# Norm boundaries of a two-layer block: another order on TensorE, ScalarE and VectorE, the next phase's first half k-outer

## Chip, core and metric

The kernel runs on one core of a Trainium2 chip. The metric is the time of the whole program on the device in microseconds (us); lower is better. The kernel before has a median of 2238.09 us over 3 runs.

## What is computed

The reference is a stack over x of 512 tokens by 1024 features, all in float32: an mLSTM mixer, a feed-forward layer, a gated spatial mixer, a feed-forward layer, then a second block with two attention branches and a convolved feed-forward layer. What matters here is what stands between any two of them:

```python
x = x + g1 * rmsnorm(y, norm_g[i, 1])
h = rmsnorm(x, norm_g[i, 2]) * (1.0 + sc2) + sh2
y = jnp.square(jax.nn.relu(h @ ffn_w1[i])) @ ffn_w2[i]
x = x + g2 * rmsnorm(y, norm_g[i, 3])
```

rmsnorm divides a token's row by the root of the mean of its squares plus 1e-6. So between the last product into y and the first product of h stand two norms in a row, each of which needs a sum over all 1024 features of a token.

## The kernel before

**Layout.** Activations are held transposed, as [128 partitions, 8 feature blocks, 512 tokens]: X (the residual), Y (the last blocks of y are summed here), h_hi and h_lo. Each float32 operand is split into a high part in a reduced format and a low rest, and each product is three matmuls (hi*hi, hi*lo, lo*hi). Weights come as 1 MB tiles of 256 columns into two slots raw[0] and raw[1], in turns. ScalarE copies a tile to its high part (`w_split`, line 1201; for the next phase's first two tiles `split_next`, line 1252, into buffers of their own) and VectorE subtracts to get the rest (`w_rest`, line 1711; `rest_of`, line 1767), which counts `split_done`.

**Queues.** The order of the work is written out by hand for each engine, with waits on counting semaphores. SyncE's queue issues the tiles in order (`tile_in`, line 368); a tile t waits for `split_done` of tile t-2, that is, until the rest of the tile that was in its slot has been computed. ScalarE and VectorE carry out their lists in order.

**A boundary.** There are five: a_out, ffn0, b_out, ffn1 and out2 (named by the phase that ends). All but out2 have two norms (`two`). The last two weight tiles of a phase are multiplied in `last_pair` (line 620), the first two of the next one in `first_pair` (line 665), or, behind ffn0, in a loop of its own (lines 933 to 950). Both split the tokens in halves of 256. In `last_pair` half 0 goes through four blocks m of 8 k steps of three products, into banks 0 to 3; then half 1 the same, into banks 4 to 7, and while half 1 is multiplied, the norms of half 0 are computed:

- VectorE's `y_out(half, m)` (line 1772) adds a block's bank to y; ScalarE squares it (`y_square`, line 1219) into T[m]; VectorE adds the square into sq_sum (`y_sum`, line 1787).
- TensorE's `sums` (line 598) multiplies sq_sum by a column of ones; `variance` (line 1796, VectorE), `half_power` (line 2536, GpSimd: the power -1/2), `diagonal` (line 1802, VectorE) and `spread_half` (line 615, TensorE) turn it into the reciprocal root of each token on all partitions, in a bank.
- `merge` (line 1810) computes x = x + y * gain * that, a block at a time. In half 1 GpSimd does every second add (line 2550). ScalarE squares x (`x_squares`, line 1235), `x_sums` (line 606) sums on TensorE, and the chain variance, power, diagonal, spread follows once more.
- `h_parts` (line 1825): VectorE scales a block of x into T, ScalarE makes h_hi (`hi`, line 1254), VectorE the rest h_lo (line 1829) and counts `h_ready`.

All the small products of the statistics stand at fixed places in TensorE's list: in `last_pair` those of half 0 at the steps (half, m, k) in the code, in the next phase's first half those of half 1, by `norm_step(name, i, k)` (line 652). `first_pair` runs s (the tile) outermost, then k, then two banks. Its half 1 waits for `h_ready1` k by k.

The lists of ScalarE and VectorE at the head of a boundary, which the change touches:

```python
split_next(0)                 # ScalarE, lines 1264 to 1268
for m in range(3):
    y_square(m, y[m], hs[0])
split_next(1)
y_square(3, y[3], hs[0])
```

```python
y_out(0, 2)                   # VectorE, lines 1851 to 1857
y_sum(0, 2)
y_out(0, 3)
y_sum(0, 3)
rest_of(t2, 1, next_w[name][1], 2, lambda: variance(0, 9 * kb_ + 1))
diagonal(0, 2 * kb_)
spread_done(0, 2 * kb_)
```

## Time and profile before

| | us |
|---|---|
| median of 3 runs | 2238.09 |
| lowest, highest | 2231.41, 2239.53 |
| the profiled execution's own time | 2227.2 |
| its span, first to last instruction | 2225.4 |
| TensorE busy | 2123.7 (95% of the span) |
| VectorE, ScalarE, GpSimd busy | 1230.6, 826.0, 95.9 |
| mean granted TensorE clock | 0.981 of full speed |

Matmuls are pipelined: the profile's duration of one is longer than the distance between two starts, so distances are read from starts. A float32 product with 128x1 or with `diag` shows as two records. "Idle before" is time in which the engine did nothing, with the instruction that ended it. Times of a row count from the start of the span; the boundaries stand at 266 to 348 (a_out), 668 to 737 (ffn0), 984 to 1053 (b_out), 1358 to 1422 (ffn1) and 1816 to 1866 us (out2).

### The profile page before, as it was taken

The numbers are of one execution on the slowest core, as the hardware profiler recorded it, in microseconds if no ns is written. First come the engines' busy times: TensorE is split into PE (matmuls) and PEld (weight loads), VectorE is DVE, ScalarE is ACT, GpSimd is POOL, SyncE is SP. The second block draws the span as 40 slices with busy tenths as digits, with TensorE's granted clock in tenths as the row PEclk, the third lists the DMA queues.
The fourth block names the chain that finished last, engine by engine and source line by source line (L and its number), as shares of the span: only waits on it lengthen the run. The fifth ranks groups of instructions, "written<-read, shape, count | busy, mean of one in ns | idle before, by whom it ended". The sixth has DMA issues, their size and how long they took to land.

```text
span 2225.4 us, 29809 instructions
## 1 busy us (share of the span) xinstructions
PE 2123.7 (95%) x11614; PEld 1777.6 (80%) x11614; DVE 1230.6 (55%) x1994; ACT 826.0 (37%) x1229; POOL 95.9 (4%) x71
## 2 busy tenths in 40 slices
PE   6999879999999999999999999999999999999997
PEld 5897768888888998788888888886666689888886
DVE  4666667666667445647333336535557756535455
ACT  3433334334244322325342343336445534424243
POOL 0000010000001002401000000100000000000000
PEclk9999989999999999999999999999999999999999
DMA  9451314666551432231223323222012131222221
GB/s 293 152 190 48 110 56 159 203 210 196 194 188 59 151 96 91 79 114 57 76 95 95 112 91 96 63 69 85 1 48 77 47 112 60 94 95 94 95 85 67
DMA packets 224630, 239.34 MB, mean 108 GB/s; under 512 B 6642, under 2 KB 219021, under 8 KB 223877
## 3 DMA queue, kind: packets, MB, share of 16 engines
q1 hardware_dynamic: 182757, 193.73, 27.1%
q10 hardware_dynamic: 41760, 44.06, 6.0%
q8 instruction: 76, 1.25, 0.2%
q14 instruction: 37, 0.30, 0.0%
HBM read 230.81 MB, written 6.31 MB: 107 GB/s over the span
## 4 chain that ended last, share of the span: by engine, by line
PE 66%; issue 18%; DVE 7%; DMA 3%; ACT 3%; DVEq 1%; POOL 1%; SPq 1%; ACTq 0%; POOLq 0%
PE bank L546 43%; PE bank L1133 4%; PE bank L686 2%; DMA ada_raw<-in_ada_w 2%; PE bank L740 2%; PE bank L644 2%; DVE ada_acc L1722 2%; PE bank L1081 1%; PE bank L1070 1%; PE bank L1028 1%; PE bank L1058 1%; PE bank L1104 1%; PE bank L1116 1%; ACT w_hi L1201 1%; PE bank L611 1%
## 5 line engine op out<-in xcount | busy, mean ns | idle before, releaser
L1711 DVE TENSOR_TENSOR w_lo<-raw,w_hi 128x2048 fp32r<-128x2048 f32 x137 | 314.6, 2296 | 246.2 <-ACT w_hi L1201 246.1
L546 PE MATMUL bank<-h_hi,w_hi 128*128 128x512 f32 x1056 | 413.7, 392 | 0.0
L546 PE MATMUL bank<-h_hi,w_lo 128*128 128x512 f32 x1056 | 411.7, 390 | 0.0
L546 PE MATMUL bank<-h_lo,w_hi 128*128 128x512 f32 x1056 | 411.6, 390 | 0.0
L1201 ACT ACTIVATE w_hi<-raw 128x2048 fp32r<-128x2048 f32 x147 | 280.1, 1905 | 314.4 <-PE bank L546 308.1
L546 PE MATMUL bank<-g_hi,w_hi 128*128 128x512 f32 x688 | 271.3, 394 | 9.4 <-DVE g_lo L2498 5.1
L546 PE MATMUL bank<-g_hi,w_lo 128*128 128x512 f32 x688 | 269.6, 392 | 0.0
L546 PE MATMUL bank<-g_lo,w_hi 128*128 128x512 f32 x688 | 269.4, 392 | 0.0
L546 PEld LDWEIGHTS bank<-h_hi,w_lo 128*128 128x128 f32 x1056 | 198.7, 188 | 41.6
L546 PEld LDWEIGHTS bank<-h_lo,w_hi 128*128 128x128 f32 x1056 | 198.8, 188 | 41.1 <-issue 0.2
L546 PEld LDWEIGHTS bank<-h_hi,w_hi 128*128 128x128 f32 x1056 | 198.7, 188 | 40.7 <-issue 0.2
L546 PEld LDWEIGHTS bank<-g_hi,w_hi 128*128 128x128 f32 x688 | 130.3, 189 | 37.7 <-DVE g_lo L2498 6.4
L546 PEld LDWEIGHTS bank<-g_hi,w_lo 128*128 128x128 f32 x688 | 130.1, 189 | 27.4
L546 PEld LDWEIGHTS bank<-g_lo,w_hi 128*128 128x128 f32 x688 | 130.2, 189 | 26.7
L1722 DVE SCALAR_TENSOR_TENSOR ada_acc<-ada_raw,c_act,ada_acc 128x256 f32<-128x256 f32 x280 | 135.8, 485 | 21.5 <-issue 0.6
L2197 DVE TENSOR_TENSOR g_lo<-tmp,g_hi 128x512 fp32r<-128x512 f32 (+1 forms) x72 | 44.5, 630 | 127.9 <-ACT g_hi L1454 127.8
L1448 ACT ACTIVATE tmp<-bank 128x512 f32<-128x512 f32 (+1 forms) x72 | 39.4, 547 | 163.7 <-PE bank L546 163.1
L546 PE MATMUL bank<-w_hi,h_hi 128*128 128x256 f32 x352 | 100.0, 284 | 0.0
L546 PE MATMUL bank<-w_lo,h_hi 128*128 128x256 f32 x352 | 99.6, 283 | 0.0
L546 PE MATMUL bank<-w_hi,h_lo 128*128 128x256 f32 x352 | 99.6, 283 | 0.0
L1906 DVE TENSOR_TENSOR y_acc<-y_acc,bank 128x512 f32<-128x512 f32 x60 | 40.8, 684 | 88.7 <-PE bank L546 88.7
L644 PE MATMUL bank<-g_hi,w_hi 128*128 128x256 f32 x256 | 78.5, 307 | 1.4 <-DVE w_lo L1711 1.1
(415 smaller groups left out, 3668.9 us busy)
## 6 DMA issues: line engine op xcount, KB each, us to landing
raw<-in_ffn_w SPq DMA_DIRECT2D x64, 1024.0 KB, 5.2
ada_raw<-in_ada_w ACTq DMA_DIRECT2D x40, 1024.0 KB, 5.2
raw<-in_w_up SPq DMA_DIRECT2D x22, 1024.0 KB, 5.0
raw<-in_b_w_in SPq DMA_DIRECT2D x16, 1024.0 KB, 5.3
raw<-in_w_in SPq DMA_DIRECT2D x15, 1024.0 KB, 5.6
raw<-in_a_w_in SPq DMA_DIRECT2D x12, 1024.0 KB, 5.5
ada_head<-in_ada_w SPq DMA_DIRECT2D x8, 1024.0 KB, 11.8
raw<-in_b_w_out SPq DMA_DIRECT2D x8, 1024.0 KB, 5.2
```

The lines of the kernel that those rows point to most:

```text
L546: mm = pe.matmul(o, x, y, start=(k == 0 and j == 0), stop=(k == kc - 1 and j == 2))
L611: mm = pe.matmul(bank[4 * half + 1][:, c:c + 1], xsq[:, b, c * P:c * P + P], ones[:, 0:1], start=(b == 0 and c == 0), stop=(b == KB - 1 an ...
L644: mm = pe.matmul(bank[4 * half + m][:, hs], x, y, start=(k == 0 and j == 0), stop=(k == KB - 1 and j == 2))
L686: mm = pe.matmul(o, x, y, start=(k == 0 and j == 0), stop=(k == KB - 1 and j == 2))
L740: mm = pe.matmul(bank[6][:], x, y, start=(k == 0 and j == 0), stop=(k == KB - 1 and j == 2))
L1133: mm = pe.matmul(bank[7][:], x, y, start=(k == 0 and j == 0), stop=(k == KB - 1 and j == 2))
L1201: act.activation(w_hi[s][:], raw[s][:], ACT.Copy).then_inc(sem("hi_done"), 1)
L1448: r = act.activation(t, i[:, hs], ACT.Relu)
L1711: dve.tensor_tensor(w_lo[s][:], raw[s][:], f32(w_hi[s][:]), ALU.subtract).then_inc(sem("split_done"), 1)
L1722: i = dve.scalar_tensor_tensor(o, src[:, k], c_act[:, k:k + 1], o, ALU.mult, ALU.add)
L1906: dve.tensor_tensor(y, y, bank[m][:], ALU.add).then_inc(sem(f"evac{m}"), 1)
L2197: return dve.tensor_tensor(g_lo[:, y, hs], T[m][:, hs], f32(g_hi[:, y, hs]), ALU.subtract)
```

## The change

It reorders the boundaries. Banks of the statistics are named by `norm_banks`: (0, 0, 1, 4) for half 0 and (5, 5, 6, 7) for half 1 where there are two norms. On TensorE the statistics move, `sums` takes the fourth square straight from T[3], and `x_sums` goes by pairs of blocks:

```diff
+def sums(name, half):
+    kb_, o = BOUNDS[name], bank[norm_banks(name, half)[0]]
+    for i, sq in enumerate([sqa, T[3]]):
+        if i == 0:
+            pe.wait_ge(sem(f"sq_ready{half}"), 5 * kb_ + 1)
+        else:
+            pe.wait_ge(sem("y_squared"), 12 * kb_ + 8 + 4 * half)
+        for c in range(2):
+            mm = pe.matmul(o[:, c:c + 1], sq[:, half * HALF + c * P:half * HALF + c * P + P],
+                           ones[:, 0:1], start=(i == c == 0), stop=(i == c == 1), skip_group_check=True)
     mm.then_inc(sem(f"sq_used{half}"), 1)
...
-                    sums(0, 9 * kb_, sqa)
-                if (half, m, k) == (1, 1, 2):
-                    spread_half(0, 2 * kb_)
-                if two and (half, m, k) == (1, 3, 2):
-                    x_sums(name, 0, range(4, KB))
-                if two and (half, m, k) == (1, 3, 7):
-                    spread_half(0, 2 * kb_ + 1)
+                if (half, m, k) == (1, 0, 3):
+                    sums(name, 0)
+                if (half, m, k) == (1, 0, 7):
+                    spread_half(name, 0)
+                if two and (half, m, k) == (1, 2, 2):
+                    x_sums(name, 0, (2, 3))
+                if two and (half, m, k) == (1, 2, 6):
+                    spread_half(name, 0, True)
...
-            if two and (half, m) == (1, 2):
-                x_sums(name, 0, range(4))
...
-def norm_step(name, i, k):
-    kb_ = BOUNDS[name]
-    two = name != "out2"
-    if (i, k) == (0, 4):
-        sums(1, 9 * kb_, sqa)
-    if (i, k) == (0, 7) and two or (i, k) == (1, 2) and not two:
-        spread_half(1, 2 * kb_)
-    if (i, k) == (1, 3) and two:
-        x_sums(name, 1, range(3))
-    if (i, k) == (1, 6) and two:
-        x_sums(name, 1, range(3, KB))
+            if two and (half, m) == (1, 1):
+                x_sums(name, 0, (0, 1))
+def norm_step(name, k):
+    if k == 1:
+        sums(name, 1)
+    if k == 2:
+        spread_half(name, 1)
+    if k in (4, 5):
+        x_sums(name, 1, (k - 4,))
+    if k == 6:
+        x_sums(name, 1, (2, 3))
+    if k == 7:
+        spread_half(name, 1, True)
```

`first_pair` runs its first half with k outermost over four banks (banks 0 to 3), and so does the loop behind ffn0, with bank 2s+i taking token quarter i of each half; out2's keeps its order:

```diff
+    for k in range(KB):
+        norm_step(name, k)
+        pe.wait_ge(sem("h_ready0"), 8 * BOUNDS[name] + k + 1)
+        for m in range(4):
+            step(0, m // 2, m % 2, k, bank[m], True)
+    for s in range(2):
+        for k in range(KB):
+            if s == 0:
+                pe.wait_ge(sem("h_ready1"), 8 * BOUNDS[name] + k + 1)
+            for b in range(2):
+                step(1, s, b, k, bank[4 + 2 * s + b], True)
...
+for k in range(KB):
+    norm_step("ffn0", k)
+    pe.wait_ge(sem("h_ready0"), 8 * BOUNDS["ffn0"] + k + 1)
     for i in range(2):
...
+        b_in_step(0, i, k)
+for i in range(2):
+    for k in range(KB):
+        if i == 0:
+            pe.wait_ge(sem("h_ready1"), 8 * BOUNDS["ffn0"] + k + 1)
+        b_in_step(1, i, k)
```

ScalarE:

```diff
-    def x_squares(half):
-        for b in range(KB):
-            if half:
-                act.wait_ge(sem("x_odd" if b % 2 else "x_even"), 4 * kb_ + b // 2 + 1)
-                if b == 0:
-                    act.wait_ge(sem("sq_used0"), 9 * kb_ + 9)
...
-            else:
-                act.wait_ge(sem("x_ready0"), 8 * kb_ + b + 1)
-            act.activation(xsq[:, b], X[:, b, hs[half]], ACT.Square).then_inc(sem(f"sq_ready{half}"), 1)
+    def x_squares(half, i):
+        act.wait_ge(sem(f"x_ready{half}"), 4 * kb_ + i + 1)
+        if half and i == 0:
+            act.wait_ge(sem("sq_used0"), 5 * kb_ + 5)
+        act.activation(xsq[:, 2 * i:2 * i + 2], X[:, 2 * i:2 * i + 2, hs[half]], ACT.Square)\
+           .then_inc(sem(f"sq_ready{half}"), 1)
...
     split_next(0)
-    for m in range(3):
+    y_square(0, y[0], hs[0])
+    split_next(1)
+    for m in range(1, 4):
         y_square(m, y[m], hs[0])
-    split_next(1)
-    y_square(3, y[3], hs[0])
     if two:
-        x_squares(0)
-        for m in range(3):
-            y_square(m, y[m], hs[1])
-        hi(0, range(3))
+        for i in range(4):
+            x_squares(0, i)
+        y_square(0, y[0], hs[1])
+        y_square(1, y[1], hs[1])
+        w_split(u + 1, 0, 4 * q + 2)
+        hi(0, range(2))
+        y_square(2, y[2], hs[1])
+        hi(0, (2,))
         y_square(3, y[3], hs[1])
-        hi(0, range(3, KB))
-        w_split(u + 1, 0, 4 * q + 2)
-        x_squares(1)
+        hi(0, range(3, 6))
+        x_squares(1, 0)
+        x_squares(1, 1)
+        hi(0, (6,))
+        x_squares(1, 2)
+        x_squares(1, 3)
+        hi(0, (7,))
         w_split(u + 1, 1, 4 * q + 4)
         hi(1, range(KB))
```

The first four gelu's behind ffn0 follow that bank layout with a strided output. VectorE, helpers (`TT[i]` is T[2i] and T[2i+1] as one tensor) and order; `y_sum` of m = 3 is gone, and m = 2 releases the sums:

```diff
+    def merge(half, i):
+        t = TT[i % 2]
+        for b in range(2):
+            dve.scalar_tensor_tensor(t[:, b, hs[half]], Y[:, 2 * i + b, hs[half]], y_gain_[:, 2 * i + b:2 * i + b + 1],
+                                     bank[norm_banks(name, half)[1]][:, 0:HALF], ALU.mult, ALU.mult)
+        dve.drain()
+        x = X[:, 2 * i:2 * i + 2, hs[half]]
+        dve.tensor_tensor(x, x, t[:, :, hs[half]], ALU.add).then_inc(sem(f"x_ready{half}"), 1)
```

```diff
     y_out(0, 0)
     rest_of(t2, 0, next_w[name][0], 1)
     y_out(0, 1)
     y_sum(0, 0)
+    rest_of(t2, 1, next_w[name][1], 1)
+    y_out(0, 2)
     y_sum(0, 1)
-    y_out(0, 2)
     y_sum(0, 2)
     y_out(0, 3)
-    y_sum(0, 3)
-    rest_of(t2, 1, next_w[name][1], 2, lambda: variance(0, 9 * kb_ + 1))
-    diagonal(0, 2 * kb_)
-    spread_done(0, 2 * kb_)
+    variance(0)
+    diagonal(0)
+    spread_done(0)
     if two:
-        merge(0, range(KB))
-        for m in range(3):
-            y_out(1, m)
+        for i in range(4):
+            merge(0, i)
+        y_out(1, 0)
+        y_out(1, 1)
         y_sum(1, 0)
+        variance(0, True)
         y_sum(1, 1)
-        variance(0, 9 * kb_ + 9, 1)
+        diagonal(0, True)
+        spread_done(0, True)
+        h_scale(0, 0)
+        h_scale(0, 1)
+        h_rest(0, 0)
+        y_out(1, 2)
+        h_scale(0, 2)
+        h_rest(0, 1)
         y_sum(1, 2)
-        diagonal(0, 2 * kb_ + 1)
-        spread_done(0, 2 * kb_ + 1)
-        h_parts(0, range(KB), {2: lambda: y_out(1, 3), 3: lambda: y_sum(1, 3),
-                               5: lambda: variance(1, 9 * kb_ + 1), 6: lambda: diagonal(1, 2 * kb_)})
-        spread_done(1, 2 * kb_)
-        merge(1, range(KB))
-        rest_of(t2 + 2, 0, (w_hi[0], w_lo[0]), 2, lambda: variance(1, 9 * kb_ + 9, 1))
-        diagonal(1, 2 * kb_ + 1)
-        spread_done(1, 2 * kb_ + 1)
+        h_rest(0, 2)
+        y_out(1, 3)
+        h_scale(0, 3)
+        h_scale(0, 4)
+        h_rest(0, 3)
+        variance(1)
+        h_scale(0, 5)
+        h_rest(0, 4)
+        diagonal(1)
+        h_rest(0, 5)
+        spread_done(1)
+        merge(1, 0)
+        merge(1, 1)
+        h_scale(0, 6)
+        h_rest(0, 6)
+        merge(1, 2)
+        merge(1, 3)
+        h_scale(0, 7)
+        h_rest(0, 7)
+        variance(1, True)
+        diagonal(1, True)
+        spread_done(1, True)
     else:
...
-        y_sum(1, 3)
-        rest_of(t2 + 2, 0, (w_hi[0], w_lo[0]), 2, lambda: variance(1, 9 * kb_ + 1))
-        diagonal(1, 2 * kb_)
-        spread_done(1, 2 * kb_)
+        rest_of(t2 + 2, 0, (w_hi[0], w_lo[0]), 2, lambda: variance(1))
+        diagonal(1)
+        spread_done(1)
+    y_count[0] += 8
     h_parts(1, range(KB))
+    if two:
+        rest_of(t2 + 2, 0, (w_hi[0], w_lo[0]), 1)
     rest_of(t2 + 2, 1, (w_hi[1], w_lo[1]), 1)
```

`h_scale` and `h_rest` are the two halves of the old `h_parts` loop, with the same operations. On GpSimd the four adds of `merge` in half 1 are removed (with their semaphores). Nothing changes in SyncE's queue.

## Rows read from the trace of the kernel before

**Rows 1.** The page: busy time of each engine, share of the span.

```profile
PE 2123.7 (95%) x11614; PEld 1777.6 (80%) x11614; DVE 1230.6 (55%) x1994; ACT 826.0 (37%) x1229; POOL 95.9 (4%) x71
```

**Rows 2.** Waits of TensorE: engine, line, waited for, total us, times, longest.

```profile
PE bank L686 <- DVE h_lo L1829: 11.9, 18, 1.6
PE bank L602 <- DVE sq_sum L1792: 7.3, 5, 4.5
```

**Rows 3.** Windows: length, busy us by engine, granted TensorE clock, DMA share, GB/s.

```profile
1009.60:1016.40 6.80, 6.80 (x32) 6.62 (x32) 2.74 (x7) 1.21 (x4) 0.70 (x1) 0.51 0.00 0
286.90:290.40 3.50, 3.50 (x15) 3.25 (x15) 3.27 (x5) 0.42 (x1) 0.00 (x0) 0.50 0.00 0
685.50:688.70 3.20, 3.20 (x16) 3.17 (x15) 1.95 (x4) 0.00 (x0) 1.61 (x1) 0.50 0.11 29
1380.00:1386.00 6.00, 6.00 (x54) 6.00 (x54) 4.94 (x14) 2.68 (x7) 0.70 (x1) 1.00 0.00 0
```

**Rows 4.** Timeline of TensorE, ffn1: start, us, what, idle before and releaser.

```profile
1357.76 0.28 PE L644 MATMUL bank<-g_hi,w_hi 128*128 128x256 f32 x1
...
1371.20 0.56 PE L602 MATMUL bank<-ones,sq_sum 128*128 128x1 f32 x4
...
1380.06 1.84 PE L611 MATMUL bank<-ones,x_squares 128*128 128x1 f32 x16
...
1388.61 0.36 PE L686 MATMUL bank<-h_hi,ffn_next_hi 128*128 128x256 f32 x1 [1.22 <-DVE h_lo L1829]
...
1422.16 0.40 PE L546 MATMUL bank<-h_hi,w_hi 128*128 128x512 f32 x1
```

**Rows 5.** Timeline of VectorE, ffn1.

```profile
1359.40 0.69 DVE L1917 TENSOR_TENSOR sq_sum<-sq_sum,tmp 128x512 f32<-128x512 f32 x1 [0.74 <-ACT tmp L1223]
...
1366.17 0.41 DVE L1780 TENSOR_TENSOR y_acc<-y_acc,bank 128x256 f32<-128x256 f32 x1
1366.77 0.93 DVE L1792 TENSOR_TENSOR sq_sum<-sq_sum,tmp 128x256 f32<-128x256 f32 x2 [0.19 <-issue]
...
1374.02 0.42 DVE L1805 TENSOR_TENSOR diag<-cst_sb,rstd 128x256 f32<-128x256 f32 x1 [0.59 <-POOL rstd L2539]
1375.24 0.48 DVE L1816 SCALAR_TENSOR_TENSOR tmp<-y_acc,ycol,bank 128x256 f32<-128x256 f32 x1 [0.79 <-PE bank L617]
...
1377.03 0.47 DVE L1816 SCALAR_TENSOR_TENSOR tmp<-y_acc,ycol,bank 128x256 f32<-128x256 f32 x1
...
1387.07 0.87 DVE L1833 SCALAR_TENSOR_TENSOR tmp<-x_res,vcols,bank 128x256 f32<-128x256 f32 x2 [0.79 <-PE bank L617]
```

**Rows 6.** Timelines of VectorE and TensorE, b_out.

```profile
1001.94 0.48 DVE L1816 SCALAR_TENSOR_TENSOR tmp<-y_acc,ycol,bank 128x256 f32<-128x256 f32 x1 [0.79 <-PE bank L617]
...
1018.23 0.36 PE L686 MATMUL bank<-h_hi,b_out_next_hi 128*128 128x256 f32 x1 [1.29 <-DVE h_lo L1829]
...
1053.10 0.40 PE L546 MATMUL bank<-h_hi,w_hi 128*128 128x512 f32 x1
```

**Rows 7.** Line 371, the queue of the tiles, ffn1: issue and landing.

```profile
L371 SPq DMA_DIRECT2D raw<-in_w_in x1: 378/378/378, 1363.5 to 1363.5; - x1
DMA to landing us min/median/max: 4.7/4.7/4.7
```

**Rows 8.** Timeline of ScalarE, the second split in ffn0, b_out, out2.

```profile
682.01 1.91 ACT L1252 ACTIVATE ffn_next_hi<-raw 128x2048 fp32r<-128x2048 f32 x1 [0.68 <-DMA raw<-in_b_w_in]
...
995.11 1.91 ACT L1252 ACTIVATE b_out_next_hi<-raw 128x2048 fp32r<-128x2048 f32 x1 [0.42 <-DMA raw<-in_ffn_w]
...
1826.80 1.91 ACT L1252 ACTIVATE out_next_hi<-raw 128x2048 fp32r<-128x2048 f32 x1 [0.40 <-DMA raw<-in_w_up]
```

**Rows 9.** Timeline of ScalarE, ffn1.

```profile
1363.90 0.42 ACT L1223 ACTIVATE tmp<-y_acc 128x256 f32<-128x256 f32 x1 [0.93 <-DVEq L1785]
...
1368.44 1.90 ACT L1252 ACTIVATE ffn_next_hi<-raw 128x2048 fp32r<-128x2048 f32 x1
```

**Rows 10.** Line 2539, the powers on GpSimd: ns least, median, most, first and last start.

```profile
L2539 POOL TENSOR_TENSOR rstd<-var,neghalf x18: 696/1607/1622, 296.3 to 1847.6; 128x2 f32<-128x2 f32 x18
```

More of the change, by code:

```diff
@@ new lines, in x_sums @@
+            def x_sums(name, half, pairs):
+                kb_, o = BOUNDS[name], bank[norm_banks(name, half)[2]]
+                for i in pairs:
+                    pe.wait_ge(sem(f"sq_ready{half}"), 5 * kb_ + i + 2)
+                    for b in (2 * i, 2 * i + 1):
+                        for c in range(2):
+                            mm = pe.matmul(o[:, c:c + 1], xsq[:, b, c * P:c * P + P], ones[:, 0:1],
+                                           start=(b == 0 and c == 0), stop=(b == KB - 1 and c == 1), skip_group_check=True)
@@ L665, in first_pair, with step @@
+            def norm_step(name, k):
[9 more added lines that the diff above has]
+                    spread_half(name, 1, True)
             def first_pair(name, t, q):
-                one_bank = name == "out2"
-                for half in range(2):
+                def step(half, s, b, k, o, last):
@@ L689, in first_pair @@
-                    if half == 0 and not one_bank:
-                        spread_half(1, 2 * BOUNDS[name] + 1)
+                    wh, wl = (w[:, k * 256 + b * P:k * 256 + b * P + P] for w in next_w[name][s])
+                    for j, (x, y) in enumerate([(wh, h_hi[:, k, hs]), (wh, h_lo[:, k, hs]), (wl, h_hi[:, k, hs])]):
+                        mm = pe.matmul(o[:, hs], x, y, start=(k == 0 and j == 0), stop=(k == KB - 1 and j == 2))
+                    if k == KB - 1 and last:
+                        mm.then_inc(sem("block_done" if half else "half_done"), 1)
@@ new lines, in first_pair @@
+                for s in range(2):
+                    pe.wait_ge(sem("split_done"), t + s + 1)
+                for m in range(4):
+                    evacuated(m, q)
+                if name == "out2":
+                    for half in range(2):
+                        for s in range(2):
+                            for k in range(KB):
+                                if (half, s, k) == (0, 0, 4):
+                                    sums(name, 1)
+                                if (half, s, k) == (0, 1, 2):
+                                    spread_half(name, 1)
+                                if s == 0:
+                                    pe.wait_ge(sem(f"h_ready{half}"), 8 * BOUNDS[name] + k + 1)
+                                for b in range(2):
+                                    step(half, s, b, k, bank[2 * s + b], half == 1)
+                    return
@@ L2533, in boundary @@
                 kb_ = BOUNDS[name]
-                hs = slice(HALF, S)
                 def half_power(half, n):
```

150 lines of the change are left out of this document (55 added, 95 removed).

## The prediction

> **What bounds the kernel now.** The page comes first: TensorE is busy for 95% of the span [rows 1], so the change can only give back idle or slow TensorE time. The waits of TensorE come next [rows 2]. At the norm boundaries it waits 11.9 us for rows of h (line 686, the first pair of three of them) and 7.3 us for the sum of squares (line 602, all five): 19 us, 0.9% of the span. Beside some smaller waits only the clock is in the change's reach besides. The windows show the clock [rows 3]: in b_out the granted clock is 0.51 (the 1.2 GHz level) for the 6.8 us from 1009.6 on, after a stretch of 128x1 statistics products with no idle time in it. In a_out, behind a long idle stretch, it is 0.50, and 15 products fill 3.5 us, 0.213 us from start to start.
>
> Then I follow ffn1 on TensorE [rows 4]. From 1357.76 to 1371.20 run 111 products, 0.121 us each; 16 records of 128x1 products take 1.84 us, of which the last overlaps the next product by 0.12 (1.72; half as many 0.86). I call **M** the first merge (1375.24 [rows 5]) and **E** the first full-width product behind the boundary (1422.16 [rows 4]). M to E is 46.9 us in ffn1 and 51.2 us in b_out [rows 6]; the same two places are 47.7 us apart in a_out and in ffn0. Together 193.5 us.
>
> **Step 1: the second tile's split moves ahead of three squares.** ScalarE's list was split(0), squares 0 to 2, split(1), square 3. Now split(1) stands behind square 0, and on VectorE its rest (2.2 us) stands ahead of y_out(0,2). What decides is when the tile is there. Its transfer can be issued only when the slot's last rest is done: 1363.5, landing 4.7 us later, at 1368.2 [rows 7]. In three other boundaries ScalarE waits for that very transfer, until 682.0, 995.1 and 1826.8 [rows 8]. No line of the transfers' queue changes, so these times stay. Call the split's start S. Its rest can start at S+1.93 (1.9 us [rows 9] and a handover) and ends at S+4.14, where y_out(0,2) begins. y_out(0,3) stands 1.35 us later: y_out to sum is 0.60 us and two sums take 0.85 (the second of them waits 0.1 for its square) [rows 5], S+5.5. Its square starts 0.49 us later and takes 0.40 [rows 5, 9]. So the sums can start at **S+6.4**. In ffn1 that is 1374.7, where before they ran at 1371.20. Moreover TensorE now stands in front of them after 105 products, at 1370.5: it waits 4.2 us. In b_out it is 1001.5 against 997.8 (wait 4.9), in ffn0 688.4 against 684.7 (wait 6.1), in out2 1833.2 against 1829.5 (wait 4.8). In a_out the tile has long landed, since VectorE was late with other work: its sums move by +0.5 only. Leaving square 3 out of the VectorE sum saves 0.4 us, and is in the 6.4.
>
> Such a wait brings the low clock: a_out's idle stretch did, and so did 1.55 us at the sums in ffn0, behind which 3.2 us ran at 0.50 [rows 3].
>
> **Step 2: sums to merge.** Now no rest stands between them, and the power on GpSimd has nothing beside it: 0.70 us, the shortest of its 18 runs, instead of their median, 1.61 [rows 10]. At full clock: 0.60 (sums to variance) + 0.23 + 0.73 (power) + 1.22 (diagonal to merge [rows 5]) = 2.8 us against 4.04 before [rows 4, 5]. At the low clock TensorE itself is late with the 12 products in front of the spread: 0.9 + 2.56 + 0.9 = 4.35. The floor is +2.2 us for M, the low-clock value +3.5 to +3.9. I take the second, as the waits are longer than the 1.55 us that sufficed: ffn1 +3.6, b_out +3.9, ffn0 +3.5, a_out -0.3. **Sum +10.7.**
>
> **Step 3: merge to E at full clock.** Merging in pairs: two scaled rows start 0.39 us apart, then one add of 512 columns at 0.69 us: 1.55 us a pair with the drain between, where two rows took 1.79 [rows 5]. The last x squares end at M+6.95. TensorE needs the first half of them at M+3.0 and gets them at M+3.85, and the second half at M+6.3 and gets them at M+6.95: waits of 0.9 and 0.65, a new pair of stalls. 1.72 for the products and 1.5 for variance, power and diagonal give the second spread at M+10.2; 30 products are left, so the next phase begins at **F = M+14.25** (before 13.4, 1388.61 [rows 4]). By then rows of h are ready (M+12.5): the 1.2 to 1.4 us at its head and the five waits of 0.2 to 0.35 inside go, the point of running k outermost, 1.45 us a row. The second half's x: y_out(1,3) at F+0.35, sums, power and spread put the first merge at F+4.55; two merges, one row of h (1.7 us, its high part waits for a square on ScalarE), two merges and the last squares end at F+13.2. TensorE asks for them at F+11.8: it waits 1.4 us. Then 1.72, row 6, spread, row 7 end at F+18.3; the half's first row of h is ready at F+18.7; seven rows at VectorE's 0.79 us and 48 products end at F+30.8. So E = M+45.05, four times 180.2 against 193.5: **-13.3**. The moved rest of the next tile ends at F+28.3, before E, and costs nothing; if its cover goes, 2.2 us. GpSimd's four adds, 0.73 us each, no longer carry x; the added sums products (0.4 us) run inside the wait.
>
> **Step 4: the clock in the statistics stretches.** From M+3.0 to M+8.7 TensorE has 3.4 us of 128x1 products, 1.5 us of waits and 0.7 us of real ones. Before, the same products with the same real ones between them and no waits dropped the clock once in four boundaries, and that boundary needed 16.3 us from M to its first product of the next phase [rows 3, 6] where 13.4 is usual: 2.9 us. Below, a late drop costs only the 12 products, 1.1. I take 2.0 us, nearer the middle because the new stretch is poorer in each boundary. The second stretch (F+11.8 to F+14.9) costs 0 or, with 12 products slow, 1.4: I take 1.0. Four times 3.0: **+12.0**.
>
> The Trainium skill (TensorE: Matmul & The Clock Gate, Why this matters for your kernels) names only idle gaps between bursts as what sends the clock down; b_out's drop has no idle gap, so the row stands against the page. By that rule the +12.0 would be 0.
>
> **Step 5: out2.** It is TensorE-bound from end to end: it gets the wait of 4.8 us and 1.3 us of low clock, and loses its old waits of 0.3, 0.85 and 0.6. **+4.3.** The b_in blocks and the gelu in another order change no work: nothing.
>
> Sum: 10.7 - 13.3 + 12.0 + 4.3 = **+13.7 us**. Against the profiled execution (2227.2 us, its span 2225.4) that is 2240.9; that execution lies 10.9 below the median of the runs, 2238.09, to which I add it, rounded down: **2251 us**.
>
> **Rivals.** (a) *Statistics products don't drop the clock*: only step 4 falls away, +1.7, 2239.8. For it: before, the other three boundaries kept 1.00 there, as ffn1 from 1380 to 1386 [rows 3]. Against: b_out, and the added waits. It is also what the page's rule gives. 0.18. (b) *The clock stays at 2.4 GHz throughout*, after the sums too: M moves by 2.2 us in three, -0.7 in a_out, out2 by 3.0; 5.9 - 13.3 + 3.0 = -4.4, 2233.7, not slower. It is decided at the first products behind the sums (granted clock 1.00 or 0.50). Against: both drops after idling. 0.09. (c) *The tile is there when square 0 is done*: no wait at the sums. M then moves by -1.9, -2.4, -3.9 and -0.3, out2 by -1.3, and steps 3 and 4 bring -1.3: -11, 2227. Against it are four landing times. 0.12. (d) *The low level holds through both statistics stretches*: 2.9 and 1.4 in each boundary, +19, 2257, and one more stall behind it could make 2260. 0.15. The forecast itself has 0.46 and its own range is 2245 to 2258.
>
> **Chances.** A measurement of this kernel can tell about 0.5%, 11.2 us. Slower by more: 0.37 of the forecast's 0.46, and (d): 0.52. Within: (a), (b), the forecast's remaining 0.09 and 0.02 of (c): 0.38. Faster by more: the other 0.10 of (c). The range leaves out most of (c) and the end of (d): 2233 to 2260.
>
> **What would show it.** Right: in four boundaries line 1252's second split still waits for its transfer, TensorE idles 4 to 6 us in front of the sums and runs at 0.50 behind them; the power takes 0.70; a pair of merges 1.55; no waits for h in the first half of the next phase; waits of about 1 us at the x sums; M to E near 48. Wrong: sums within a microsecond of where they were, or M to E under 45.

## The result, and the profile after

Over 17 runs each the changed kernel takes 2245.19 us (median; 2236.62 to 2248.2), the kernel before 2231.46 us (2228.03 to 2239.53). The ratio of the means is 1.0052, 95% interval 1.0041 to 1.0062: 11.6 us slower. The two medians lie 13.7 us apart; the 11.6 is used below, since the times in the boundaries add up to it. The forecast was 13.7 us slower, 2251 us.

The page of the changed kernel (TensorE first, then the others: busy us, share of the span, instructions), against [rows 1]:

```profile
PE 2142.0 (95%) x11654; PEld 1800.0 (80%) x11654; DVE 1226.9 (55%) x1959; ACT 819.6 (37%) x1197; POOL 72.3 (3%) x55
```

TensorE has the same share of a span that is 18.1 us longer. Its waits (engine, line, waited for, total us, times, longest) answer to [rows 2]; L614 is the sums, L625 the x sums, L684 the first pair:

```profile
PE bank L614 <- DVE sq_sum L1827: 21.7, 5, 5.6
PE bank L625 <- ACT x_squares L1267: 2.4, 7, 0.4
PE bank L684 <- DVE h_lo L1867: 0.4, 2, 0.2
```

The 18 waits of 11.9 us for rows of h became two of 0.4 us; behind ffn0, where a loop of its own asks for them, 4.2 us became 0.2. The five waits for the sum of squares grew from 7.3 to 21.7 us. TensorE on its timeline in ffn1 (start, us, engine, line, operation, idle before and its releaser), the places of [rows 4]:

```profile
1369.18 0.28 PE L657 MATMUL bank<-g_hi,w_hi 128*128 128x256 f32 x1
...
1385.34 1.01 PE L614 MATMUL bank<-ones,sq_sum 128*128 128x1 f32 x4 [3.28 <-DVE sq_sum L1827]
...
1405.87 0.28 PE L684 MATMUL bank<-h_hi,ffn_next_hi 128*128 128x256 f32 x1
...
1435.31 0.40 PE L553 MATMUL bank<-h_hi,w_hi 128*128 128x512 f32 x1
```

T, the start of `last_pair`, is 1369.18, and the sums stand at T+16.16 where they stood at T+13.44. ScalarE and VectorE show why, on their timelines of the same stretch:

```profile
1379.59 1.92 ACT L1277 ACTIVATE ffn_next_hi<-raw 128x2048 fp32r<-128x2048 f32 x1 [3.85 <-DMA raw<-in_w_in]
...
1384.24 0.42 ACT L1251 ACTIVATE tmp<-y_acc 128x256 f32<-128x256 f32 x1 [2.43 <-DVEq L1821]
1385.70 0.42 ACT L1251 ACTIVATE tmp<-y_acc 128x256 f32<-128x256 f32 x1 [1.04 <-DVEq L1821]
```

```profile
1381.54 2.29 DVE L1803 TENSOR_TENSOR ffn_next_lo<-raw,ffn_next_hi 128x2048 fp32r<-128x2048 f32 x1 [2.92 <-ACT ffn_next_hi L1277]
1383.75 0.41 DVE L1816 TENSOR_TENSOR y_acc<-y_acc,bank 128x256 f32<-128x256 f32 x1
1384.36 0.93 DVE L1827 TENSOR_TENSOR sq_sum<-sq_sum,tmp 128x256 f32<-128x256 f32 x2 [0.20 <-issue]
1385.20 0.41 DVE L1816 TENSOR_TENSOR y_acc<-y_acc,bank 128x256 f32<-128x256 f32 x1
1387.24 0.16 DVE L1836 TENSOR_SCALAR var<-bank 128x2 f32<-128x2 f32 x1 [1.63 <-PE bank L614]
1388.21 0.43 DVE L1843 TENSOR_TENSOR diag<-cst_sb,rstd 128x256 f32<-128x256 f32 x1 [0.81 <-POOL rstd L2598]
1390.87 0.87 DVE L1852 SCALAR_TENSOR_TENSOR tmp_pair<-y_acc,ycol,bank 128x256 f32<-128x256 f32 x2 [2.23 <-PE bank L631]
1391.81 0.69 DVE L1856 TENSOR_TENSOR x_res<-x_res,tmp_pair 128x512 f32<-128x512 f32 x1
1392.42 0.87 DVE L1852 SCALAR_TENSOR_TENSOR tmp_pair<-y_acc,ycol,bank 128x256 f32<-128x256 f32 x2
```

The second split begins when its tile lands, at 1379.59; the rest follows; only then come y_out(0,2), at T+14.6, and y_out(0,3), at T+16.0, with the squares of blocks 2 and 3. TensorE had finished their banks at T+8.9 and T+11.8. The first merge M is at T+21.69, before it was at T+17.48 [rows 4, 5]. Two merges and their add are 1.55 us apart. The powers on GpSimd (ns: least, median, most):

```profile
L2598 POOL TENSOR_TENSOR rstd<-var,neghalf x18: 695/696/1607, 303.8 to 1866.8; 128x2 f32<-128x2 f32 x18
```

The clock, in windows (length; busy us of TensorE, its loads, VectorE, ScalarE, GpSimd; granted clock; DMA share; GB/s). The first three stand behind the sums and in the x statistics of ffn1, the next in the x statistics of b_out, ffn0 and a_out:

```profile
1385.40:1391.00 5.60, 5.60 (x24) 5.42 (x25) 0.94 (x4) 0.42 (x1) 0.70 (x1) 0.50 0.56 183
1392.00:1398.50 6.50, 6.50 (x58) 6.44 (x57) 5.99 (x13) 3.20 (x7) 0.00 (x0) 1.00 0.00 0
1399.00:1402.20 3.20, 3.20 (x15) 3.11 (x15) 1.00 (x3) 1.31 (x1) 0.70 (x1) 0.50 0.00 0
1023.60:1030.00 6.40, 6.32 (x27) 6.14 (x28) 2.49 (x7) 2.79 (x5) 0.70 (x1) 0.50 0.00 0
706.10:712.30 6.20, 6.20 (x27) 6.02 (x28) 2.28 (x7) 2.59 (x4) 0.70 (x1) 0.50 0.00 0
313.90:320.00 6.10, 6.05 (x26) 5.87 (x27) 2.19 (x7) 2.49 (x4) 0.70 (x1) 0.50 0.01 1
```

The same places read in all five boundaries, in us, from starts on the timelines. M, E and F are those of the prediction (the first merge, the first full-width product behind the boundary, the start of the next phase), and T is the start of `last_pair`:

| | T to sums, before / after | T to M | M to F | F to E | T to E |
|---|---|---|---|---|---|
| a_out | 28.82 / 28.58 | 33.95 / 33.86 | 13.53 / 16.30 | 34.21 / 31.43 | 81.69 / 81.59 |
| ffn0 | 16.45 / 18.66 | 20.95 / 24.19 | 13.52 / 16.51 | 34.18 / 31.42 | 68.65 / 72.12 |
| b_out | 13.92 / 17.25 | 18.02 / 22.78 | 16.29 / 16.42 | 34.87 / 31.43 | 69.18 / 70.63 |
| ffn1 | 13.44 / 16.16 | 17.48 / 21.69 | 13.37 / 15.00 | 33.55 / 29.44 | 64.40 / 66.13 |
| out2 | 13.90 / 16.80 | | | 24.79 / 24.35 | 50.48 / 55.54 |

The last column adds up to 334.40 before and 346.01 after: +11.6 us, the measured difference. Each kernel has one profiled execution, so every entry is one reading. The profiled execution of the changed kernel is 6.5 us longer than this explains (2243.5 against 2225.4). It lost 6.9 us ahead of a_out, where the two kernels have the same instructions; the kernels of the experiments, which have them too, came there at 267.5 to 274.8. So the sums over boundaries are the better reading, and kernels are compared by them here.

### The profile page after: what moved, and what is told of

Same layout as the page of the kernel before. It is cut to its first block, busy times and chain, and to the rows that moved or that the text cites. A ratio compares the mean times of both kernels' runs of the same rounds, so it can differ in the third digit from the quotient of the medians.

```text
span 2243.5 us, 29780 instructions
## 1 busy us (share of the span) xinstructions
PE 2142.0 (95%) x11654; PEld 1800.0 (80%) x11654; DVE 1226.9 (55%) x1959; ACT 819.6 (37%) x1197; POOL 72.3 (3%) x55
## 4 chain that ended last, share of the span: by engine, by line
PE 67%; issue 18%; DVE 7%; DMA 3%; ACT 3%; DVEq 1%; SPq 1%; ACTq 0%; POOL 0%; POOLq 0%
PE bank L553 43%; PE bank L1161 4%; PE bank L684 2%; PE bank L657 2%; PE bank L765 2%; DMA ada_raw<-in_ada_w 2%; PE bank L1109 1%; DVE ada_acc L1758 1%; PE bank L1098 1%; PE bank L1056 1%; PE bank L1086 1%; PE bank L1144 1%; PE bank L1132 1%; DVE x_res L1856 1%; PE bank L964 1%
## 5 line engine op out<-in xcount | busy, mean ns | idle before, releaser
L657 PE MATMUL bank<-g_hi,w_hi 128*128 128x256 f32 x256 | 83.1, 325 | 1.4 <-DVE w_lo L1747 1.1
```

The source lines that it names most:

```text
L657: mm = pe.matmul(bank[4 * half + m][:, hs], x, y, start=(k == 0 and j == 0), stop=(k == KB - 1 and j == 2))
```

## The experiments

Theory A: the place of the second tile's split and rest costs 12.1 us ahead of the first merges and 5.1 in out2; behind the merge the change gains. Rival B: the loss lies in the new statistics stretches. Ratios are to the kernel before on the same chip. The table at the end of this section has the boundaries of every run.

### The head as before (e1)

```diff
     split_next(0)
-    y_square(0, y[0], hs[0])
+    for m in range(3):
+        y_square(m, y[m], hs[0])
     split_next(1)
-    for m in range(1, 4):
-        y_square(m, y[m], hs[0])
+    y_square(3, y[3], hs[0])
...
-    rest_of(t2, 1, next_w[name][1], 1)
-    y_out(0, 2)
     y_sum(0, 1)
+    y_out(0, 2)
     y_sum(0, 2)
     y_out(0, 3)
-    variance(0)
+    rest_of(t2, 1, next_w[name][1], 2, lambda: variance(0))
     diagonal(0)
```

> The changed kernel with the head of the boundary as before: the second tile's split behind the square of block 2, its rest in two pieces behind y_out(0,3) with the variance between them. Theory A (the place of split and rest costs what was lost: the changed kernel's first merges stand 12.1 us later in the four two-norm boundaries together, and out2 takes 5.1 us more, while from the first merge on the boundaries are 5.6 us shorter): TensorE's waits for the sums fall from 4.5, 4.4, 3.3 and 3.9 us to 2.3, 1.2, 0.4 and 0.8 us (ffn0, b_out, ffn1, out2), and the kernel takes about 15 us less than the changed one: ratio to before 0.998 (0.996 to 0.999). Rival B (the loss is in the new statistics stretches behind the first merge): the ratio stays at 1.004 or above. If short waits of 0.4 to 1.2 us still bring the 1.2 GHz level, half of the gain stays away: ratio 1.001.

Measured: 0.9949 (0.993 to 0.9968), faster than either kernel. The gain over the changed kernel is larger than expected (0.998, range 0.996 to 0.999): 22 us in the boundaries. The waits of TensorE, and the window from the sums to the merge in b_out:

```profile
PE bank L631 <- DVE diag L1843: 4.0, 4, 1.0
PE bank L614 <- DVE sq_sum L1827: 3.7, 1, 3.7
PE bank L614 <- ACT tmp L1251: 1.4, 3, 0.6
```

```profile
996.20:1001.00 4.80, 3.49 (x27) 3.15 (x26) 2.92 (x5) 0.75 (x2) 1.62 (x1) 1.00 0.23 73
```

Except in a_out there is no wait for sq_sum left. The product with T[3] waits 1.4 us in all for the square of block 3, and the spreads wait about 1 us each for the diagonal, since the power again has the rest beside it (1.62 us in this window). TensorE idled 1.3 of these 4.8 us and kept 2.4 GHz (granted clock 1.00). These short waits did not bring the low level; behind the 3.3 to 5.6 us of the changed kernel it was there in every boundary. Theory A holds; B would have stayed at 1.004.

### The head alone (e2)

The other way round: the kernel before with the same two lists in the changed order.

```diff
     split_next(0)
-    for m in range(3):
-        y_square(m, y[m], hs[0])
+    y_square(0, y[0], hs[0])
     split_next(1)
-    y_square(3, y[3], hs[0])
+    for m in range(1, 4):
+        y_square(m, y[m], hs[0])
...
-    y_sum(0, 1)
+    rest_of(t2, 1, next_w[name][1], 1)
     y_out(0, 2)
+    y_sum(0, 1)
     y_sum(0, 2)
     y_out(0, 3)
     y_sum(0, 3)
-    rest_of(t2, 1, next_w[name][1], 2, lambda: variance(0, 9 * kb_ + 1))
+    variance(0, 9 * kb_ + 1)
```

> The kernel before with only the second tile's split moved behind the square of block 0 and its rest ahead of y_out(0,2). Theory A: the sums can start 6.1 to 6.5 us after the second split's start, T+17 instead of T+13.4 in ffn1, TensorE waits 3 to 5 us for them in four boundaries, and the products behind run at the 1.2 GHz level; 3 times 4.9 and out2 5.0 us: +17 to +20 us, ratio 1.008 (1.006 to 1.010). Rival B: below 1.003, since the old order has slack behind the first merge that takes it up.

Measured: 1.0104 (1.0085 to 1.0124), a little above the expected range, 22 us more in the boundaries. The sums' waits and the product behind one:

```profile
PE bank L602 <- DVE sq_sum L1792: 24.3, 6, 5.6
PE bank L686 <- DVE h_lo L1829: 12.0, 18, 1.6
```

```profile
1387.78 1.01 PE L602 MATMUL bank<-ones,sq_sum 128*128 128x1 f32 x4 [3.90 <-DVE sq_sum L1792]
```

ffn1's sums are at T+17.50, as expected. The waits for h are still those of before: this part alone costs 22 us, so all the rest of the change is worth 10.4 (22.0 less 11.6); e1, with the rest alone, has 10.6.

### The rest behind everything (e3, e11)

If the second tile is not wanted before the next phase, nothing on the way to the merge should wait for it.

```diff
     split_next(0)
-    y_square(0, y[0], hs[0])
-    split_next(1)
-    for m in range(1, 4):
+    for m in range(4):
         y_square(m, y[m], hs[0])
+    split_next(1)
...
-    rest_of(t2, 1, next_w[name][1], 1)
     y_out(0, 2)
...
         diagonal(0, True)
+        rest_of(t2, 1, next_w[name][1], 1)
         spread_done(0, True)
...
         y_sum(1, 1)
+        rest_of(t2, 1, next_w[name][1], 1)
         h_parts(0, range(4, KB))
```

> The changed kernel with the second tile's split behind all four squares and its rest behind the diagonal of the second norm (in out2 behind the first sums of half 1), where VectorE idles 2.1 us in the profile of the changed kernel. Theory A: nothing waits for the second tile ahead of the sums any more; they start at T+13.0, a wait of 0.3 us, the power takes 0.70 us, the first merge stands 2.8 us behind the sums at T+15.9 (20.9 in ffn0 with the changed kernel's 24.2 is the worst, 17.5 in the kernel before in ffn1). 5 to 6 us less than the changed kernel in each of three boundaries, 6 in ffn0, 0 to 1 in a_out, 5 in out2: about -22 us against the changed kernel, ratio to before 0.995 (0.993 to 0.997). Rival B: the ratio stays above 1.000. Rival C (the rest in its new place holds up the rows of h): as A, but each next phase begins 2.2 us later, ratio 0.998.

Measured: 0.9924 (0.9904 to 0.9944), more of a gain than expected (0.993 to 0.997). TensorE and VectorE in ffn1 (T is 1349.60):

```profile
1362.32 0.50 PE L614 MATMUL bank<-ones,sq_sum 128*128 128x1 f32 x4
1362.69 0.58 PE L614 MATMUL bank<-ones,tmp 128*128 128x1 f32 x4
...
1364.76 0.70 PE L631 MATMUL bank<-diag,ones 128*128 128x256 f32 x2
```

```profile
1365.49 0.87 DVE L1851 SCALAR_TENSOR_TENSOR tmp_pair<-y_acc,ycol,bank 128x256 f32<-128x256 f32 x2 [0.79 <-PE bank L631]
...
1374.65 0.42 DVE L1842 TENSOR_TENSOR diag<-cst_sb,rstd 128x256 f32<-128x256 f32 x1 [0.26 <-POOL rstd L2598]
1374.99 2.28 DVE L1802 TENSOR_TENSOR ffn_next_lo<-raw,ffn_next_hi 128x2048 fp32r<-128x2048 f32 x1
1377.19 0.87 DVE L1859 SCALAR_TENSOR_TENSOR tmp<-x_res,vcols,bank 128x256 f32<-128x256 f32 x2
```

The sums run at T+12.72 without a wait, the merge is at T+15.89. The rest lies between the diagonal and the scaling of h, which starts right behind it. The next phase begins 15.01 us behind the merge, as in the changed kernel, not 2.2 later: rival C falls here. (In both kernels the clock is low in this stretch; e9 below shows the stretch without it.) Each boundary from T to E is 4.2 to 9.8 us shorter than in the changed kernel, 32 us in all.

In out2 the rest stood badly: three short waits, 25.90 us from F to E instead of 24.35. e11 moves only that one behind out2's first diagonal:

```diff
     diagonal(0)
+    if not two:
+        rest_of(t2, 1, next_w[name][1], 1)
     spread_done(0)
...
-        rest_of(t2, 1, next_w[name][1], 1)
         h_parts(0, range(4, KB))
```

> As e3, with only out2's second rest moved directly behind the first diagonal. In e3 out2 waits 0.43, 0.20 and 0.25 us in half 0 of the next phase and takes 25.9 us there instead of 24.35. Expected: T to E in out2 49.0 to 49.7 us instead of 50.6, ratio 0.992 (0.9915 to 0.9925); e5's 0.9894 was then mostly its x statistics and not this edit. Rival: the whole of e5's gain over e3 was here, ratio 0.990.

Measured: 0.9913 (0.9891 to 0.9936), out2 49.72 us. The size is as expected. The ratio is not told apart from e3's.

### The same placing in the kernel before (e8)

```diff
     split_next(0)
-    for m in range(3):
+    for m in range(4):
         y_square(m, y[m], hs[0])
     split_next(1)
-    y_square(3, y[3], hs[0])
...
     y_sum(0, 3)
-    rest_of(t2, 1, next_w[name][1], 2, lambda: variance(0, 9 * kb_ + 1))
+    variance(0, 9 * kb_ + 1)
     diagonal(0, 2 * kb_)
+    if not two:
+        rest_of(t2, 1, next_w[name][1], 1)
...
     diagonal(0, 2 * kb_ + 1)
+    rest_of(t2, 1, next_w[name][1], 1)
```

> The kernel before with the same placing of split and rest as in e3 (split behind all four squares, rest behind the diagonal of the second norm, in out2 behind the first diagonal), all else as before. If what e3 gained is the placing alone, this one comes to e3's ratio, 0.992. By the traces so far it saves T to M only: sums at T+13.4 against 13.4 to 16.5 and 2.8 us to the merge against 4.0 to 4.5, so 1.2 us in ffn1, 1.7 in b_out, 3 in ffn0, 0 to 2 in a_out, -0.5 to 1 in out2, while from the merge to the end of the pair it keeps 46.9 to 51.2 us plus whatever of the 2.2 us rest is not hidden: 5 to 8 us less than before, ratio 0.997 (0.995 to 0.999), so that half or more of e3's gain is the rest of the change.

Measured: 0.9985 (0.9968 to 1.0002); less than expected, and no gain that is clear. T to M is 6.4 us shorter in the four boundaries, M to E 7.8 us longer. TensorE's longest wait for h was 1.6 [rows 2]; now:

```profile
PE bank L686 <- DVE h_lo L1828: 13.1, 18, 2.7
PE bank L945 <- DVE h_lo L1828: 5.5, 6, 2.7
```

In the old order the first row of h is wanted sooner, and the rest in front of it makes it late: TensorE waits 2.7 us for it in a_out and ffn0, where it was 1.4. That is 2.6 of the 7.8 us. Another 2.6 are waits of 0.87 us for a diagonal of half 1 in three boundaries that had none, and 2.8 stand in ffn1, where the granted clock fell to 0.50 for 6.8 us from 1387.6 on, as it had not before; whether the edit is the reason for that fall is open. So the placing pays only together with the rest of the change: from the old head of the boundary it takes 9.7 us off there (e1 323.8, e3 314.1) and adds 2.5 here (334.4, 336.9).

### k outermost (e4)

```diff
-    for k in range(KB):
-        norm_step(name, k)
-        pe.wait_ge(sem("h_ready0"), 8 * BOUNDS[name] + k + 1)
-        for m in range(4):
-            step(0, m // 2, m % 2, k, bank[m], True)
+    for s in range(2):
+        for k in range(KB):
+            if k % 2 == 0:
+                norm_step(name, 4 * s + k // 2)
+            if s == 0:
+                pe.wait_ge(sem("h_ready0"), 8 * BOUNDS[name] + k + 1)
+            for b in range(2):
+                step(0, s, b, k, bank[2 * s + b], True)
```

> The changed kernel with half 0 of the next phase's first pair again tile by tile (not in the phase behind ffn0, whose loop stays as changed), the statistics at the same counts of products. Theory D (k outermost is what makes room for x between rows of h): row k is needed 0.73 us apart instead of 1.45; rows 6 and 7 of h, ready 9 and 13 us after the phase begins, are now wanted at 4.4 and 5.1 us: TensorE waits about 4 us for each, 8 us in each of a_out, b_out and ffn1: +20 us or more against the changed kernel, ratio to before 1.014. Rival E (the order of k and tiles does not matter, as the waits for x in the same stretch are what binds): within 0.3% of the changed kernel, ratio 1.005.

Measured: 1.0194 (1.0168 to 1.022). The waits of the first pair, and two of them on the timeline in a_out:

```profile
PE bank L684 <- DVE h_lo L1870: 21.4, 8, 3.7
```

```profile
333.04 0.39 PE L684 MATMUL bank<-h_hi,a_out_next_hi 128*128 128x256 f32 x1 [3.44 <-DVE h_lo L1870]
...
337.71 0.58 PE L684 MATMUL bank<-h_hi,a_out_next_hi 128*128 128x256 f32 x1 [3.70 <-DVE h_lo L1870]
```

Rows 6 and 7 are waited for 3.44 and 3.70 us, as theory D had it. M to E is 10.5, 7.2 and 11.9 us longer in a_out, b_out and ffn1, and not longer in ffn0, whose loop was left. About 21 of these 29.6 us are the waits. From the first of them on the clock was also low for longer than in the changed kernel; in a_out:

```profile
334.30:347.90 13.60, 10.19 (x48) 10.19 (x48) 2.58 (x6) 3.46 (x4) 0.00 (x0) 0.50 0.00 1
```

### What takes the clock down in the x statistics (e5, e6, e7, e9, e10)

In e3 TensorE's clock fell at the end of the x statistics of half 0 in all four boundaries. All these kernels share the head of e3; e5, e9 and e10 have out2's second rest where e11 has it. e5 sums x in four groups of eight records, each behind its squares:

```diff
+    XAT = [(1, 1, 7), (1, 2, 0), (1, 2, 2), (1, 2, 4)]
...
-    if two and (half, m, k) == (1, 2, 2):
-        x_sums(name, 0, (2, 3))
-    if two and (half, m, k) == (1, 2, 6):
+    if two and (half, m, k) in XAT:
+        x_sums(name, 0, (XAT.index((half, m, k)),))
+    if two and (half, m, k) == (1, 3, 1):
         spread_half(name, 0, True)
...
-    if two and (half, m) == (1, 1):
-        x_sums(name, 0, (0, 1))
```

> The kernel with split and rest behind the squares (e3), with the x statistics of half 0 in four groups of eight 128x1 records, 3, 6 and 6 products between them and each behind its squares, and in out2 the second rest directly behind the first diagonal. In e3 the granted clock fell to 0.50 in four of four boundaries right at the end of these statistics, for 3.3 to 6.5 us, behind waits of 0.43 to 0.45 us. If it is the bunching of the 128x1 products or the waits beside them that brings the low level, it stays at 1.00 here, the next phase begins 14.2 us behind the first merge instead of 15.0 to 16.5, and with 1.5 us from out2 the kernel takes 6 us less than e3: ratio to before 0.990 (0.988 to 0.992). If it is the share of such products in the stretch, the clock falls as in e3 and only out2's part comes: ratio 0.992.

> As e3, but the x statistics leave out the odd blocks, so half of their 128x1 products (4 records a pair instead of 8), with the squares and all waits for them kept, the waits a little longer. Theory F (the 128x1 products bring the low level): granted clock 1.00 through both statistics stretches of every boundary. Theory G (the short waits do): it falls to 0.50 as in e3, behind waits of 0.4 to 1.3 us.

The edit of e6 is `for b in (2 * i,)` in place of `for b in (2 * i, 2 * i + 1)` in `x_sums`: it leaves out half of the squares of x, so its results are not the block's, and only its times are read. That of e7:

```diff
-    if two and (half, m, k) == (1, 2, 2):
+    if two and (half, m, k) == (1, 2, 7):
         x_sums(name, 0, (2, 3))
-    if two and (half, m, k) == (1, 2, 6):
+    if two and (half, m, k) == (1, 3, 3):
         spread_half(name, 0, True)
```

> As e3, but the last two pairs of x squares of half 0 are summed 15 products later, all sixteen records in one go and without a wait, the spread at the same distance behind. Theory F: the low level comes all the same, at the end of the sixteen records, and the next phase begins 15 to 16.5 us behind the first merge. Theory G: 1.00 through the first stretch in all four boundaries, the next phase 14.2 us behind the first merge, ratio to before 0.991.

Measured: e5 0.9894 (0.9872 to 0.9916), e6 0.9895 (0.9864 to 0.9926, two runs), e7 0.9924 (0.9897 to 0.995). Windows of e5 in ffn1, the stretch with the four groups and the one behind it:

```profile
1364.40:1370.80 6.40, 6.40 (x58) 6.36 (x56) 6.11 (x13) 2.05 (x4) 0.00 (x0) 1.00 0.00 0
1370.90:1377.30 6.40, 6.40 (x31) 6.40 (x31) 3.89 (x7) 2.86 (x4) 0.69 (x1) 0.50 0.00 0
```

TensorE was busy for all of the first 6.4 us at 2.4 GHz, and the next 6.4 ran at 1.2 (granted clock 0.50). The same came in ffn0. In a_out and b_out this stretch kept 1.00, but there the clock fell 4.4 and 4.2 us into the next phase. So e5's ratio is the one expected for a clock that stays up, while the clock did not stay up. No wait is needed for the low level. Two kernels read above show that as well: the changed one in ffn1 (6.50 of 6.50 us busy from 1392.00, then 0.50), and e3 in a_out, where the x sums, other than the expectation of e5 has it, waited for nothing:

```profile
309.00:315.10 6.10, 6.10 (x55) 6.10 (x54) 5.25 (x13) 3.35 (x7) 0.00 (x0) 1.00 0.01 3
315.25:318.60 3.35, 3.35 (x16) 3.17 (x15) 3.00 (x4) 1.19 (x1) 0.70 (x1) 0.50 0.01 2
```

e6 in ffn1, and e7 in ffn1 (the last sixteen records and what follows) and b_out:

```profile
1366.00:1371.00 5.00, 3.56 (x27) 3.18 (x27) 4.46 (x11) 3.16 (x6) 0.45 (x1) 1.00 0.00 0
1371.20:1374.20 3.00, 3.00 (x14) 2.81 (x14) 2.92 (x3) 0.88 (x1) 0.05 (x1) 0.50 0.03 5
```

```profile
1372.00:1379.00 7.00, 6.59 (x53) 6.17 (x52) 4.83 (x8) 3.12 (x5) 0.70 (x1) 1.00 0.00 0
1007.00:1012.00 5.00, 4.34 (x33) 3.92 (x32) 4.05 (x7) 1.10 (x3) 0.70 (x1) 1.00 0.00 0
```

In e6, with half of the 128x1 products, the low level came in four of four boundaries, in ffn1 behind a stretch in which TensorE idled 1.4 of 5 us. In e7, with all of them, no wait among them and 15 more real products between the two groups of sixteen, it stayed away from this stretch in four of four. Neither theory F (the products) nor theory G (the waits) is right alone, and what decides stays open. What goes with the kept clock is the number of real products between the two groups: with 9, 12 or 15 more of them (e9, e10, e7) it stayed up in 12 of 12 boundaries, with the groups where the change puts them (e3, e11) in none of 8. But e7 gained nothing. Its spread stands 15 products later, and TensorE waited 1.1 to 1.3 us for the first row of h in each boundary.

e9 takes a middle place, (1, 2, 5) and (1, 3, 1), with out2 as in e11; e10 takes (1, 2, 6) and (1, 3, 2), and sums the first two pairs of half 1 together at k = 5:

> As e3 with the second rest of out2 directly behind the first diagonal, and the last two pairs of x squares of half 0 summed 9 products later than in e3 (6 earlier than in e7), the spread 12 products behind them. In e7 the granted clock stayed at 1.00 through this stretch in four of four boundaries, but the next phase waited 1.26 us for its first row of h, so nothing came of it. Here the fourth pair is ready by the time it is asked for (6.95 us behind the merge, asked for at 7.4), so no wait, and the wait for the first row of h falls to 0.5 us. If the clock stays up: M to F 13.7 to 14.2 us, 1 to 2 us less than e3 in each of four boundaries and 1 to 1.5 in out2: ratio 0.989. If it falls as in e3: 0.992.

> As e9, but 3 products later still, and in half 1 the first two pairs of x squares together at k = 5 instead of one each at k = 4 and 5. First stretch: clock at 1.00 as in e7, wait for h 0.9 us, M to F 14.0 to 14.4. Second stretch (in e7 0.50 for 3 to 4 us in a_out and b_out, 1.00 in ffn0 and ffn1): if bunching the products ahead of the wait brings the low level more often, 0.50 in three or four boundaries and ratio 0.991; if it is neutral, 0.989 to 0.990.

Measured: e9 0.9903 (0.9883 to 0.9923), e10 0.9912 (0.9891 to 0.9933). e9 in ffn1's first stretch, and behind the start of the next phase in b_out, with the wait at its head:

```profile
1371.00:1377.00 6.00, 5.80 (x45) 5.39 (x45) 4.73 (x9) 2.82 (x4) 0.70 (x1) 1.00 0.06 2
1015.60:1018.60 3.00, 2.77 (x11) 2.45 (x11) 2.01 (x5) 0.02 (x1) 0.00 (x0) 0.50 0.03 5
```

```profile
1010.53 0.36 PE L684 MATMUL bank<-h_hi,b_out_next_hi 128*128 128x256 f32 x1 [0.54 <-DVE h_lo L1866]
```

The first stretch kept 2.4 GHz in four boundaries of both kernels, and M to F fell to 13.6 to 14.5 us in e9. But in a_out and b_out the clock then fell 4.3 and 4.8 us into the next phase, behind the waits for h (0.55) and the last square (0.60) and about the time of the one for the diagonal. The same waits stand in e9's ffn0, where it stayed up there; e3 and e11 have none of these drops. With the clock up, rival C comes true in part: from the rest on VectorE has at most 0.2 us of idle time up to the first row of h (ffn1, b_out), and TensorE waits 0.39 to 0.55 us for that row. M to F is 55.7 us in four boundaries against 61.8 in e11, F to E 127.7 against 120.7. What the statistics stretch no longer loses is given back behind F. In e10 it is the same in a_out and b_out. Both ratios lie above the 0.989 expected of a clock that stays up, though their intervals reach it. The second stretch, in half 1, fell to 0.50 in a_out and b_out in e7, in ffn0 in e9, in ffn0 and b_out in e10, so what the bunching there does can't be told.

Times in the boundaries (us, read as above) beside the ratios:

| | T to M, four | M to E, four | out2, T to E | sum | ratio |
|---|---|---|---|---|---|
| before | 90.4 | 193.5 | 50.5 | 334.4 | 1 |
| changed | 102.5 | 188.0 | 55.5 | 346.0 | 1.0052 |
| e1 head as before | 86.3 | 187.1 | 50.4 | 323.8 | 0.9949 |
| e2 head alone | 106.0 | 194.7 | 55.7 | 356.4 | 1.0104 |
| e3 rest last | 81.2 | 182.3 | 50.6 | 314.1 | 0.9924 |
| e4 tile outermost | 102.3 | 216.0 | 56.1 | 374.5 | 1.0194 |
| e5 spaced | 81.3 | 184.8 | 49.7 | 315.8 | 0.9894 |
| e6 half the products | 81.1 | 181.1 | 50.6 | 312.8 | 0.9895 |
| e7 later, no wait | 81.0 | 185.4 | 50.6 | 317.0 | 0.9924 |
| e8 before, rest last | 84.0 | 201.4 | 51.5 | 336.9 | 0.9985 |
| e9 middle | 81.0 | 183.4 | 49.7 | 314.1 | 0.9903 |
| e10 later | 80.8 | 186.0 | 49.7 | 316.6 | 0.9912 |
| e11 e3, out2 mended | 80.9 | 182.5 | 49.7 | 313.1 | 0.9913 |

e5, e9, e10 and e11 lie within 0.2% of each other in ratio, with intervals of that size on either side, and in another order in the boundaries. Which of them is fastest is open. All are 0.9 to 1.1% faster than the kernel before and, by the two ratios, 1.4 to 1.6% faster than the changed one. e11 is the simplest.

## Why the prediction was right

The sign, the size and the way of the loss were right: 13.7 us forecast, 11.6 measured. Part of the closeness is luck: T to M came out 1.4 us and out2 0.8 us dearer than forecast, M to E 4.3 us cheaper. The time itself, 2251 us against 2245.19, is 5.8 us off, nearly all of it because the forecast was added to the median of three runs, 2238.09, which lies 6.6 us above that of 17.

**Step 1** (the sums wait for the second tile) held in the four boundaries for which it forecast such a wait. There the split waits for its transfer, until T+10.4 to T+12.6 (before it stood at T+10.7 to T+13.7). The waits were 3.3, 4.4, 4.5 and 3.9 us in ffn1, b_out, ffn0 and out2, against 4.2, 4.9, 6.1 and 4.8 forecast, so two of them lie under the 4 to 6 us named as a sign. The first sums product stands at S+5.75 (6.1 in ffn0), not S+6.4: the step took it to need all squares, but only the product with T[3] needs the last one (that square ends at 1386.12, S+6.5). In ffn0 the tile also came 1.2 us sooner behind T. a_out moved by -0.2, forecast +0.5. e1 and e2 show that this step is the loss: taken back it gives 22 us, alone it costs 22, with the low clock behind it in both figures.

**Step 2** (sums to merge at the low clock) was right in kind and 1.2 us short in three boundaries, 5.53 us instead of 4.35, and 0.9 in a_out (5.28). The term that was mis-sized is the sums themselves: eight records take 1.73 us at 1.2 GHz (1385.34 to 1387.07 in ffn1), and the sum had four, 0.9. It had placed the four added by T[3] inside the wait. The 12 products took 2.71, not 2.56, and spread to merge 1.09, not 0.9. T to M came to +12.1, forecast +10.7.

**Steps 3 and 4** together: M to E in four boundaries -5.6 us, forecast -13.3 + 12.0 = -1.3. At full clock F to E is 29.44 us (ffn1) and not 30.8, and four times 1.36 is 5.4 us less than worked out. The stretch behind the merge took 2.05, 2.26, 2.17 and 0.75 us more than the 14.25 forecast at full clock, 7.2 against 8.0 forecast. The second one cost 2.0 in three boundaries and nothing in ffn1, 6.0 against 4.0. The waits for h went and the pair of merges took 1.55. The waits at the x sums were at most 0.45 in half 0 (none in ffn1) and 0.32 in half 1, where the steps had 0.9, 0.65 and 1.4: that part of step 3 was too dear. So the sign of waits of about 1 us there did not show, and in ffn1 M to E was 44.4 us, under the 45 that was named as a sign of being wrong.

What lowers the clock there was left open by the prediction between waits and products. e5, e3's a_out and the changed kernel's ffn1 show it without a wait, and what decides is still open. The Trainium skill (TensorE: Matmul & The Clock Gate, Why this matters for your kernels) names idle gaps between bursts; here e5's 6.4 us without any idle time were followed by 6.4 us at 0.50, so the measurement stands against the page as b_out did before. Rival (a), 2239.8 us, had the low level stay away from these stretches; in the changed kernel it came in four of four boundaries behind the merge.

**Step 5**, out2: +5.1, forecast +4.3. The wait was 3.9 us and not 4.8, but the low level cost more than the 1.3: the eight records took 1.73 us here too and the 12 products 2.71, 4.4 us for what is 2.3 at full clock.

The power took 0.70 us in the median. The rival in which the tile is there when square 0 is done fell with the four waits for its transfer; the one in which the clock stays at 2.4 GHz fell at the products behind the sums (granted clock 0.50). Rival (d), the low level in both stretches of every boundary, nearly came true: it was in the first in four of four and in the second in three of four. Only its price of 2.9 us for the first was too high, which came to 1.8 in the mean; the 1.4 for the second came to 1.5. So step 4 is right by its sum, 13.2 us for 12.0, as a middle value between a clock that stays and one that falls.
